# Two transformer blocks in one kernel: operands of the matrix products placed at other addresses, and sums of squares added by VectorE

## The chip, the cores and the metric

The kernel runs on one core of a Trainium2 chip. The metric is the time of one execution on the device in microseconds (us); lower is better.

## The reference

Two transformer blocks are applied to one sequence of 256 tokens with 2048 features, in fp32. Cut to what matters:

```python
# block 1
mod = silu(c) @ w_ada + b_ada                      # 6 vectors of 2048
h = rms_norm(x, mix_norm_pre) * (1 + sc1) + sh1
a_q, a_f, a_i, a_g, b_q, b_k, b_v, c_a, c_g = split(h @ w_in)
ya = hgrn2_mixer(...)                              # 8 heads, a gated recurrence
yb = dilated_attention_mixer(...)                  # 12 heads, three dilations
yc = silu(layer_norm(causal_conv31(c_a * sigmoid(c_g))))
merged = sum of sigmoid(h @ w_gate) * (y @ w_out) over the three
x = x + g1 * rms_norm(merged @ w_o, mix_norm_post)
h = rms_norm(x, mlp_norm_pre) * (1 + sc2) + sh2
x = x + g2 * rms_norm(relu(h @ w_up) ** 2 @ w_down, mlp_norm_post)
# block 2: the same frame, a context of 256 tokens beside x
# mixer: bidirectional mLSTM (8 heads) and differential attention (8 heads)
y = concat(mlstm, diff) @ w_out;  x = x + g1 * rms_norm(y, g_post_mix)
y = conv_ffn(h): three-tap convolution of h @ w_up, silu(gate) * value, @ w_down
x = x + g2 * rms_norm(y, g_post_ffn)
```

Each rms_norm needs, for every token, the sum of squares over the 2048 features; the layer norm needs the sum and the sum of squares over 768.

## The kernel before

**Layout.** Features lie on the 128 partitions, tokens along the free dimension: 2048 features are 16 tiles of 128x256. All weights come as one stream of 1 MiB blocks (16 weight tiles of 128x128, or 11 in down2) through the slots of `raw`. SyncE issues the loads in the order of `SECTIONS`, where G stands for a block of the products and A for one of the modulation (w_ada, w_mod), which VectorE multiplies and reduces itself.

**Products.** A block is split in two: ScalarE writes the high part (`split_high`, L529), VectorE the low part, weight minus high (`split_low`, L1767), both fp32r, into `parts[:, b % 2]`. The operand x also has a high and a low part. TensorE adds high x high, high x low and low x high for each tile: `product` (L1030 with the high weights, L1039 with the low ones) takes 48 matmuls of 256 columns a block. `gemm_parts` (L1066, L1069) reads both parts of x as one operand of 512 columns: 16 matmuls of 512 and 16 of 256 (11 and 11 in down2). Every matmul has its own weight load. `gemm_two`, `gate_chunk` and others are the same product in other orders; `gemm_tokens` swaps the roles, so that x is loaded and the weights stream.

**Places.** `operand` (L176) lays the fp32r operands into the arena at a given offset in fp32 elements: op_h and op_hw at 4096, merged, up1, yd and up2 at 12288, ya, yb, yc, ymh and yml between 20480 and 33024. `region` (L195) gives the arena's other pieces. `parts` and `raw` begin 128 bytes past a multiple of 512, the bytes of a weight tile in a partition, and every operand 192 past one, so 64 further.

**Sums of squares.** ScalarE squares a tile (`square_part`, L497, or `square`, L485) and TensorE multiplies by the constant matrix `ones`, which adds over the partitions and gives the sum to every partition, one fp32 matmul of 128x256 a tile, added up in PSUM. `norm` (L1134) does it at once for a finished tensor, `norm_part` (L1142) for some tiles. `root` (L492, L493) makes the reciprocal root of it. In four stages one product yields a tile (two in w_out_b), and its `norm_part` stands after the next product: w_o (into sq1), down1_3 (sqd1), w_out_b (sq2) and down2_3 (sq2). The norms of x itself (`norm_x`, with `keep_warm` around it) come in five chunks. The context's norm (`norm(sqc, KT)`) runs in down1_3. In the level stage (36 levels of the recurrence beside 43 product blocks) the convolution's mean is 6 matmuls at step 19 (L1308) and its variance `norm(squares, C_TILES)` at step 22.

**Order of the work.** Each engine's instructions are written out in its own order, with semaphores between. VectorE takes, for each block, the result of the block before from PSUM (`add_halves`, L1802 and L1803, in the down rounds; L2332 in w_out_b) and splits the block two ahead. At the end of a stage come `residual` (L1817, L1818) and `modulate_tiles`.

Of the kernel before, what the change touches and what calls it, by code (L numbers as in the profile page):

```python
# [13 lines left out]
P = 128  # L14
S = 256
# [136 lines left out]
def two_blocks_kernel(nc, stream, x_t, ctx_t, vec_d, const_d, lvl_mask_d, ident_d, rel_bias, c_rows, scratch, x_keep, out_t):  # L152
    with ExitStack() as ctx:
# [37 lines left out]
        arena = sb("arena", [P, ARENA])  # L191
# [131 lines left out]
        half_out = sem("half_out")  # L323
        dve_step, act_step = sem("dve_step"), sem("act_step")
# [144 lines left out]
        def _(act):  # L469
# [166 lines left out]
            for n in range(BESIDE_LEVELS):  # L636
# [22 lines left out]
                if s == 25:  # L659
# [132 lines left out]
            for k in range(KT):  # L792
# [6 lines left out]
                if k == 2:  # L799
                    root(rstd[:, S:512], M[2][:, 0:S], D)  # L800
                if k in (4, 6, 8, 10):
                    c = k // 2 - 2
# [205 lines left out]
        def _(pe):  # L1008
            norms, wholes, sq_parts = [0], [0], [0]
# [118 lines left out]
            def norm(src, n, sums=M[2]):  # L1128

                norms[0] += 1  # L1130
                wholes[0] += 1
                pe.wait_ge(sq_ready, wholes[0])
                for k in range(n):
                    ins = pe.matmul(sums[:, 0:S], ones[:, :], src[:, k, :], start=(k == 0), stop=(k == n - 1))  # L1134
                ins.then_inc(ms_ready, 1)

            def norm_part(src, k0, k1):
# [5 lines left out]
                if k1 == KT:  # L1143
                    norms[0] += 1
                    ins.then_inc(ms_ready, 1)

# [145 lines left out]
            for n in range(BESIDE_LEVELS):  # L1292
# [11 lines left out]
                if s == 19:  # L1304

                    pe.wait_ge(conv_tap, CONV_STEPS)
                    for t in range(C_TILES):
                        ins = pe.matmul(M[2][:, S:512], ones[:, :], cy[:, t, :], start=(t == 0), stop=(t == C_TILES - 1))  # L1308
                    ins.then_inc(mean_mm, 1)
                if s == 22:  # L1310
                    norm(squares, C_TILES)
# [108 lines left out]
            for k in range(KT):  # L1420
                gemm_T(gb("w_o", k), opG, waits={KT - 1: (merged_tile, KT)} if k == 0 else {})
                if k:
                    norm_part(sq1, k - 1, k)
            norm_part(sq1, KT - 1, KT)
# [16 lines left out]
            for k in range(KT):  # L1441
                gemm_parts(gb("down1_3", k), opU1, waits=waits if k == 0 else {})
                if k == 1:
                    norm(sqc, KT)
                if k:
                    norm_part(sqd1, k - 1, k)
            norm_part(sqd1, KT - 1, KT)
# [249 lines left out]
            for n in range(8):  # L1697
                w_out_b(n)
                if n:
                    norm_part(sq2, 2 * n - 2, 2 * n)  # L1700
            norm_part(sq2, 14, 16)
# [17 lines left out]
            for k in range(KT):  # L1719
                gemm_parts(gb("down2_3", k), opU2, kt=UP2, waits=waits if k == 0 else {})  # L1720
                if k:
                    norm_part(sq2, k - 1, k)
            norm_part(sq2, KT - 1, KT)
# [3 lines left out]
        def _(dve):  # L1727
# [103 lines left out]
            def modulate_tiles(op, u, add, n):  # L1831


                for k in range(KT + 2):
                    if k < KT:
                        scaled_tile(u, k)
                    if k >= 2:
                        low_tile(op, u, add, n, k - 2)

# [96 lines left out]
            for s in range(36):  # L1936
# [25 lines left out]
                if s == 23:  # L1962
# [4 lines left out]
                conv_taps(3)  # L1967
                dve.wait_ge(lvl_mm, s + 1)
# [99 lines left out]
            for k in range(KT - 1):  # L2068
                split_low(gb("w_o", k) + 2)
            ada_made(80)  # L2070
# [40 lines left out]
            for k in range(KT):  # L2111
# [5 lines left out]
                if k == 3:  # L2117
                    inverted()
                if k in (3, 5, 7, 9):
                    t = quarter_of(hfc, k // 2 - 1)  # L2120
                    dve.tensor_tensor(t, t, over_tiles(rstd[:, S:512], 4), ALU.mult).then_inc(cu_part, 1)
                if k in (5, 7, 9, 11):
                    c = k // 2 - 2
# [201 lines left out]
            for n in range(8):  # L2325
# [8 lines left out]
                if n < 7:  # L2334
                    split_low(b + 2)
            ada_made(176)
# [9 lines left out]
            for q in range(QUARTER):  # L2346
# [24 lines left out]
                else:  # L2371
                    if q == 3:
                        gains(mod2[:, 0, 80:96], v("g_post_ffn", 0, 16), 192)
                    add_round(f"down2_{q}", down2)
            inverted()
# [146 lines left out]
```

## Time and profile before

| what | value |
| --- | --- |
| median of 3 runs | 3223.66 us (3220.96 to 3226.57) |
| profiled execution | 3211.76 us |
| its span, first to last instruction | 3210.0 us |
| TensorE (PE) busy | 3132.3 us, 98% |
| VectorE (DVE) busy | 2345.0 us, 73% |
| ScalarE (ACT) busy | 1334.3 us, 42% |
| matmul records | 24132 |
| mean granted TensorE clock | 0.994 |
| moved by DMA | 722.63 MB |

PE is TensorE's matmuls, DVE VectorE, ACT ScalarE. A number behind L is a line of the kernel. Matmuls overlap in the pipeline, so the mean duration of one is longer than the spacing from one start to the next. An fp32 matmul of 128x256 has two records, a product's matmul (fp32r) one. The granted clock is a share of TensorE's full 2.4 GHz.

### The profile page before, as it was taken

What the parts mean: (1) busy time and instruction counts of PE and PEld (TensorE: products, weight loads), DVE (VectorE), ACT (ScalarE), POOL (GpSimd) and SP (SyncE); (2) the same over time, 40 slices, a digit from 0 to 9 for tenths busy, and PEclk for the clock granted to TensorE, in tenths of its full rate; (3) what the DMA queues carried; (4) which work ended last, traced back from release to release, by engine and by line L of the source; (5) the groups of instructions that cost most, each with busy time, mean ns of one, the idle gap of its engine ahead of it and who ended that gap; (6) DMA issues with size and microseconds to landing.
All of it is one profiled execution on the core that took longest, in us unless ns stands there. A gap on an engine that the chain in (4) does not pass through costs nothing.

```text
span 3210.0 us, 55608 instructions
## 1 busy us (share of the span) xinstructions
PE 3132.3 (98%) x24132; PEld 2962.3 (92%) x24132; DVE 2345.0 (73%) x2785; ACT 1334.3 (42%) x1459; POOL 1.8 (0%) x10
## 2 busy tenths in 40 slices
PE   7999999999999999999999999999999999999998
PEld 6899999899999999999988998989889999898997
DVE  5798866688877889899857765644757666767765
ACT  3333344444444443333463334422455444343444
POOL 0000000000000000000000000000000000000000
PEclk9999999999999999999999999999999999999999
DMA  9864444498894887777745763354343475655743
GB/s 395 328 218 158 159 148 153 170 351 340 333 349 158 305 310 272 267 265 288 287 171 192 280 257 140 139 207 158 132 145 130 169 266 193 231 207 195 248 175 118
DMA packets 106417, 722.63 MB, mean 225 GB/s; under 512 B 11677, under 2 KB 15389, under 8 KB 27197
## 3 DMA queue, kind: packets, MB, share of 16 engines
q1 hardware_dynamic: 100368, 703.64, 59.0%
q10 hardware_dynamic: 5806, 15.43, 1.6%
q8 instruction: 191, 3.13, 0.4%
q14 instruction: 52, 0.43, 0.0%
HBM read 712.41 MB, written 6.55 MB: 224 GB/s over the span
## 4 chain that ended last, share of the span: by engine, by line
PE 91%; DVE 6%; ACT 1%; DMA 1%; issue 1%; ACTq 0%; DVEq 0%
PE gemm L1030 40%; PE gemm L1039 19%; PE gemm L1066 12%; PE gemm L1069 6%; PE mix L1142 1%; DVE sb_parts L1767 1%; PE mix L1030 1%; PE mix L1269 1%; PE mix L1553 1%; DMA sb_arena<-x_t 1%; PE gemm L1185 1%; DVE sb_arena L1822 1%; PE mix L1039 1%; ACT sb_parts L529 1%; PE gemm L1619 0%
## 5 line engine op out<-in xcount | busy, mean ns | idle before, releaser
L529 ACT ACTIVATE sb_parts<-sb_raw 128x2048 fp32r<-128x2048 f32 (+2 forms) x489 | 899.6, 1842 | 1504.6 <-PE gemm L1039 964.5
L1767 DVE TENSOR_TENSOR sb_parts<-sb_raw,sb_parts 128x2048 fp32r<-128x2048 f32 (+2 forms) x489 | 1072.1, 2194 | 309.3 <-PE gemm L1039 147.2
L1030 PE MATMUL gemm<-op_h,sb_parts 128*128 128x256 f32 x7232 | 874.0, 278 | 1.1 <-ACT sb_parts L529 0.6
L1030 PEld LDWEIGHTS gemm<-op_h,sb_parts 128*128 128x128 f32 x7232 | 850.9, 188 | 2.5 <-ACT sb_parts L529 1.0
L1039 PE MATMUL gemm<-op_h,sb_parts 128*128 128x256 f32 x3616 | 453.7, 278 | 0.0
L1066 PE MATMUL gemm<-op_up,sb_parts 128*128 128x512 f32 x1728 | 424.8, 396 | 11.7 <-DVE op_up L2361 11.7
L1039 PEld LDWEIGHTS gemm<-op_h,sb_parts 128*128 128x128 f32 x3616 | 433.3, 188 | 0.2 <-DVE sb_parts L1767 0.2
L1066 PEld LDWEIGHTS gemm<-op_up,sb_parts 128*128 128x128 f32 x1728 | 318.8, 189 | 75.8 <-DVE op_up L2361 13.5
L1069 PEld LDWEIGHTS gemm<-op_up,sb_parts 128*128 128x128 f32 x1728 | 221.0, 190 | 10.6
L1748 DVE CUSTOM_DVE_ANT_0 sb_raw<-sb_raw,sb_arena,sb_vec 128x2048 f32<-128x2048 f32 x96 | 224.4, 2348 | 1.5 <-DMA sb_raw<-stream 0.2
L1069 PE MATMUL gemm<-op_up,sb_parts 128*128 128x256 f32 x1728 | 223.5, 280 | 0.0
L1030 PE MATMUL gemm<-op_hw,sb_parts 128*128 128x256 f32 (+1 forms) x992 | 174.3, 333 | 0.4 <-ACT sb_parts L529 0.4
L1030 PEld LDWEIGHTS gemm<-op_hw,sb_parts 128*128 128x128 f32 x992 | 150.3, 188 | 20.2 <-ACT sb_parts L529 0.6
L1740 DVE CUSTOM_DVE_ANT_0 sb_raw<-sb_raw,sb_arena,sb_vec 128x2048 f32<-128x2048 f32 x64 | 149.8, 2345 | 0.0
L2352 DVE SCALAR_TENSOR_TENSOR sb_arena<-gemm,sb_vec,sb_arena 128x255 f32<-128x255 f32 x88 | 42.5, 483 | 135.5 <-ACT sb_arena L981 135.5
L1030 PE MATMUL gemm<-sb_parts,op_hw 128*128 128x256 f32 x1024 | 121.6, 281 | 1.4 <-ACT sb_parts L529 1.4
L1030 PEld LDWEIGHTS gemm<-sb_parts,op_hw 128*128 128x128 f32 x1024 | 120.3, 191 | 2.6 <-ACT sb_parts L529 1.6
L1802 DVE TENSOR_TENSOR sb_arena<-gemm,sb_arena 128x256 f32<-128x256 f32 x96 | 40.6, 423 | 98.6 <-PE gemm L1069 98.5
L1039 PE MATMUL gemm<-op_hw,sb_parts 128*128 128x256 f32 (+1 forms) x496 | 89.6, 333 | 0.0
L1039 PEld LDWEIGHTS gemm<-op_hw,sb_parts 128*128 128x128 f32 x496 | 75.8, 188 | 9.9
L1142 PE MATMUL mix<-sb_arena,sb_ones 128*128 128x256 f32 x256 | 70.1, 393 | 9.5 <-ACT sb_arena L497 9.3
L1747 DVE CUSTOM_DVE_ANT_0 sb_arena<-sb_raw,sb_arena,sb_vec 128x2048 f32<-128x2048 f32 x32 | 75.0, 2345 | 0.0
(353 smaller groups left out, 3386.7 us busy)
## 6 DMA issues: line engine op xcount, KB each, us to landing
sb_raw<-stream SPq DMA_DIRECT2D x597, 1024.0 KB, 5.0
sb_raw<-stream SPq DMA_DIRECT2D x64, 704.0 KB, 4.1
sb_arena<-stream SPq DMA_DIRECT2D x14, 1024.0 KB, 8.7
sb_arena<-stream SPq DMA_DIRECT2D x10, 768.0 KB, 8.6
sb_raw<-stream SPq DMA_DIRECT2D x6, 768.0 KB, 7.6
sb_arena<-c_rows ACTq DMA_DIRECT2D x3, 1024.0 KB, 8.5
bias_rows<-sb_arena ACTq DMA_DIRECT2D x1, 2304.0 KB
sb_arena<-x_t ACTq DMA_DIRECT2D x4, 512.0 KB, 19.1
```

Of the source, the lines that this page charges most:

```text
L529: act.activation(parts[:, b % 2, 0, 0:kt, :], slot_of(slot)[:, 0:kt, :], ACT.Copy).then_inc(hi_ready, 1)
L1030: ins = pe.matmul(out, l, r, start=(opens and i == 0 and x is xh), stop=False, skip_group_check=True)
L1039: ins = pe.matmul(out, l, r, start=False, stop=(i == len(terms) - 1), skip_group_check=True)
L1066: pe.matmul(out, parts[:, b % 2, 0, k, :], op[:, :, k, :], start=(k == 0), stop=False, skip_group_check=True)
L1069: ins = pe.matmul(bank(b)[:, 0:S], parts[:, b % 2, 1, k, :], op[:, 0, k, :], start=False, stop=(k == kt - 1), skip_group_check=True)
L1142: ins = pe.matmul(M[1][:, 0:S], ones[:, :], src[:, k, :], start=(k == 0), stop=(k == KT - 1))
L1740: dve.tensor_tensor_reduce(w, w, c1_row, 1.0, v("b_ada", a), ALU.mult, ALU.add, mod1[:, a:a + 1])\
L1747: step(dve.tensor_tensor_reduce(products, w, cctx_row, 1.0, v("b_mod", a), ALU.mult, ALU.add, mod2[:, 1, a:a + 1]))
L1748: dve.tensor_tensor_reduce(w, w, c2_row, 1.0, v("b_mod", a), ALU.mult, ALU.add, mod2[:, 0, a:a + 1])\
L1767: dve.tensor_tensor(parts[:, b % 2, 1, 0:kt, :], slot_of(slot)[:, 0:kt, :], parts[:, b % 2, 0, 0:kt, :].bitcast(F32), ALU.subtract).then_i ...
L1802: step(dve.tensor_tensor(acc, bank(b)[:, 0:S], acc, ALU.add))
L2352: step(dve.scalar_tensor_tensor(y[:, 1:S], src[:, 0:S - 1], w0, y[:, 1:S], ALU.mult, ALU.add))
```

## The change

Two things are changed. `placed` moves everything in the arena: operands at 4096 and above by 16 elements (64 bytes), at 12288 and above by 48 (192 bytes), so that lower operands begin 128 and upper ones 256 bytes past a multiple of a weight tile's 512 bytes, counted from `parts`. And VectorE adds squares before TensorE sees them. In w_o, down1_3, w_out_b and down2_3 `add_square` adds each new tile's squares (two tiles in w_out_b) to the first, all but the last tile's; `norm_sum` then multiplies by `ones` twice (four times in w_out_b) after the last product. `fold` halves a tensor until one tile is left, for the context's norm and for the convolution's mean and variance, and `norm_folded` is one matmul. The steps behind these move by two positions: the root and scaling of the convolution from step 23 to 25 and its silu from 25 to 27, the context's root in down1_3 from k = 2 to 4, and the scaling and splits of the context by two blocks. The last down round is written out in a loop of its own, with `gains` ahead of it as before.

```diff
+        def placed(at):
+            return at + (48 if at >= 12288 else 16 if at >= 4096 else 0)
         def operand(name, at, *dims):
-            with nc.sbuf_tensor("pad_" + name, [P, at], F32), nc.sbuf_tensor("op_" + name, [P, *dims], F32R) as t:
+            with nc.sbuf_tensor("pad_" + name, [P, placed(at)], F32), nc.sbuf_tensor("op_" + name, [P, *dims], F32R) as t:
-        arena = sb("arena", [P, ARENA])
+        arena = sb("arena", [P, placed(ARENA)])
-            flat = arena[:, at:at + n]
+            flat = arena[:, placed(at):placed(at) + n]
...
@@ scalar
-                if s == 23:
+                if s == 25:
                     act.preload_act_table_set(LN_EXP)
                     root(rstd[:, 0:S], M[2][:, 0:S], C_TILES * P)
-                if k == 2:
+                if k == 4:
                     root(rstd[:, S:512], M[2][:, 0:S], D)
...
@@ tensor
-            def norm(src, n, sums=M[2]):
+            def norm_folded(src, n):
                 norms[0] += 1
-                for k in range(n):
-                    ins = pe.matmul(sums[:, 0:S], ones[:, :], src[:, k, :], start=(k == 0), stop=(k == n - 1))
+                pe.wait_ge(folded, n)
+                pe.matmul(M[2][:, 0:S], ones[:, :], src[:, 0, :], start=True, stop=True).then_inc(ms_ready, 1)
...
+            def norm_sum(src, width, n_parts):
+                sum_adds[0] += n_parts - 2
+                sq_parts[0] += n_parts
+                pe.wait_ge(sq_sum, sum_adds[0])
+                for k in range(width):
+                    pe.matmul(M[1][:, 0:S], ones[:, :], src[:, k, :], start=(k == 0), stop=False)
+                pe.wait_ge(sq_part, sq_parts[0])
+                for k in range(KT - width, KT):
+                    ins = pe.matmul(M[1][:, 0:S], ones[:, :], src[:, k, :], start=False, stop=(k == KT - 1))
...
                 if s == 19:
-                    pe.wait_ge(conv_tap, CONV_STEPS)
-                    for t in range(C_TILES):
-                        ins = pe.matmul(M[2][:, S:512], ones[:, :], cy[:, t, :], start=(t == 0), stop=(t == C_TILES - 1))
+                    pe.wait_ge(folded, 1)
+                    pe.matmul(M[2][:, S:512], ones[:, :], squares[:, 0, :], start=True, stop=True).then_inc(mean_mm, 1)
-                if s == 22:
-                    norm(squares, C_TILES)
+                if s == 24:
+                    norm_folded(squares, 2)
...
             for k in range(KT):
                 gemm_parts(gb("down2_3", k), opU2, kt=UP2, waits=waits if k == 0 else {})
-                if k:
-                    norm_part(sq2, k - 1, k)
-            norm_part(sq2, KT - 1, KT)
+            norm_sum(sq2, 1, KT)
...
@@ vector
+            def fold(dst, src, n):
+                while n > 2:
+                    rest = n // 2
+                    step(dve.tensor_tensor(dst[:, 0:rest, :], src[:, 0:rest, :], src[:, n - rest:n, :], ALU.add))
+                    src, n = dst, n - rest
+                dve.tensor_tensor(dst[:, 0, :], dst[:, 0, :], dst[:, 1, :], ALU.add).then_inc(folded, 1)
+            def add_square(sq, width, k, seen):
+                dve.wait_ge(sq_part, seen + k + 1)
+                if k > 1:
+                    dve.wait_ge(sq_sum, sum_adds[0])
+                sum_adds[0] += 1
+                dve.tensor_tensor(sq[:, 0:width, :], sq[:, 0:width, :], sq[:, width * k:width * (k + 1), :], ALU.add).then_inc(sq_sum, 1)
...
+                if s == 17:
+                    dve.wait_ge(conv_tap, CONV_STEPS)
+                    fold(squares, cy, C_TILES)
+                if s == 23:
+                    dve.wait_ge(sq_ready, 1)
+                    fold(squares, squares, C_TILES)
...
+                if k == 0:
+                    dve.wait_ge(sq_ready, 2)
+                    fold(sqc, sqc, KT)
+                if 1 <= k < KT - 1:
+                    add_square(sqd1, 1, k, 25)
```

TensorE in down2_3, the stage's last products (mix1 is the PSUM bank of the sums, gemm0 to gemm3 those of the products). Before:

```order
L1142 MATMUL mix1<-sb_arena,sb_ones 128x256
L1066 MATMUL gemm1<-op_up2,sb_parts 128x512 x11
L1069 MATMUL gemm1<-op_up2,sb_parts 128x256 x11
L1142 MATMUL mix1<-sb_arena,sb_ones 128x256
L1066 MATMUL gemm2<-op_up2,sb_parts 128x512 x11
L1069 MATMUL gemm2<-op_up2,sb_parts 128x256 x11
L1142 MATMUL mix1<-sb_arena,sb_ones 128x256 x2
```

And of the change, where L1073 and L1076 are the product's lines and L1159 and L1162 those of `norm_sum`:

```order
L1073 MATMUL gemm1<-op_up2,sb_parts 128x512 x11
L1076 MATMUL gemm1<-op_up2,sb_parts 128x256 x11
L1073 MATMUL gemm2<-op_up2,sb_parts 128x512 x11
L1076 MATMUL gemm2<-op_up2,sb_parts 128x256 x11
L1159 MATMUL mix1<-sb_arena,sb_ones 128x256
L1162 MATMUL mix1<-sb_arena,sb_ones 128x256
```

The matmul between two blocks is gone, and behind the last product there are two as before.

VectorE at the same place, from the 13th block on. Before:

```order
L1802 TENSOR_TENSOR sb_arena<-gemm0,sb_arena 128x256
L1803 TENSOR_TENSOR sb_arena<-gemm0,sb_arena 128x256
L1767 TENSOR_TENSOR sb_parts<-sb_raw,sb_parts 128x1408
L1802 TENSOR_TENSOR sb_arena<-gemm1,sb_arena 128x256
L1803 TENSOR_TENSOR sb_arena<-gemm1,sb_arena 128x256
L1802 TENSOR_TENSOR sb_arena<-gemm2,sb_arena 128x256
L1803 TENSOR_TENSOR sb_arena<-gemm2,sb_arena 128x256
```

Of the change, where L1811 and L1812 are the half adds, L1776 the low split and L1867 `add_square`:

```order
L1811 TENSOR_TENSOR sb_arena<-gemm0,sb_arena 128x256
L1812 TENSOR_TENSOR sb_arena<-gemm0,sb_arena 128x256
L1776 TENSOR_TENSOR sb_parts<-sb_raw,sb_parts 128x1408
L1867 TENSOR_TENSOR sb_arena<-sb_arena 128x256
L1811 TENSOR_TENSOR sb_arena<-gemm1,sb_arena 128x256
L1812 TENSOR_TENSOR sb_arena<-gemm1,sb_arena 128x256
L1867 TENSOR_TENSOR sb_arena<-sb_arena 128x256
L1811 TENSOR_TENSOR sb_arena<-gemm2,sb_arena 128x256
L1812 TENSOR_TENSOR sb_arena<-gemm2,sb_arena 128x256
```

Each tile's half adds are followed by the low split two blocks ahead and then by the add of the tile's squares; the last tile has none.

## Rows read from the trace of the kernel before

**Rows 1.** The page, part 1: busy time and share of each engine.
```profile
PE 3132.3 (98%) x24132; PEld 2962.3 (92%) x24132; DVE 2345.0 (73%) x2785; ACT 1334.3 (42%) x1459; POOL 1.8 (0%) x10
```

**Rows 2.** The page, part 4: the chain that ended last, by engine.
```profile
PE 91%; DVE 6%; ACT 1%; DMA 1%; issue 1%; ACTq 0%; DVEq 0%
```

**Rows 3.** TensorE's groups by shape: line, operands, shape, count | busy, mean ns of one.
```profile
L1066 PE MATMUL gemm<-op_up,sb_parts 128*128 128x512 f32 x1728 | 424.8, 396 | 11.7 <-DVE op_up L2361 11.7
...
L1142 PE MATMUL mix<-sb_arena,sb_ones 128*128 128x256 f32 x256 | 70.1, 393 | 9.5 <-ACT sb_arena L497 9.3
```

**Rows 4.** Timeline of TensorE, up1_0 and up1_2: start us, length us, instructions, count.
```profile
1000.90 3.93 PE L1030 MATMUL gemm<-op_h,sb_parts 128*128 128x256 f32 x32
...
1403.05 3.79 PE L1030 MATMUL gemm<-op_h,sb_parts 128*128 128x256 f32 x32
```

**Rows 5.** Timeline of TensorE, down1_0.
```profile
1090.82 3.82 PE L1066 MATMUL gemm<-op_up,sb_parts 128*128 128x512 f32 x16
1094.48 2.05 PE L1069 MATMUL gemm<-op_up,sb_parts 128*128 128x256 f32 x16
...
1100.04 1.98 PE L1069 MATMUL gemm<-op_up,sb_parts 128*128 128x256 f32 x16
```

**Rows 6.** TensorE by stretch, slow ones: from:to, length, busy (records), clock, DMA share, GB/s.
```profile
109.00:231.00 122.00, 117.77 (x1057) 1.00 0.71 244
323.00:580.00 257.00, 251.92 (x2063) 0.99 0.42 150
863.00:957.00 94.00, 94.00 (x775) 1.00 0.93 349
...
2247.00:2563.00 316.00, 308.41 (x2429) 0.99 0.40 144
2800.00:2956.00 156.00, 151.37 (x1203) 0.99 0.54 195
```

**Rows 7.** TensorE by stretch, token-major products of d_v.
```profile
2199.00:2213.00 14.00, 14.00 (x119) 1.00 0.76 291
2224.00:2238.00 14.00, 14.00 (x126) 1.00 0.81 301
```

**Rows 8.** Timeline of TensorE, down1_3: the context norm.
```profile
1605.71 7.07 PE L1134 MATMUL mix<-sb_arena,sb_ones 128*128 128x256 f32 x32
```

**Rows 9.** Timeline of TensorE: warming matmuls before the norm of x.
```profile
2420.38 4.63 PE L1151 MATMUL mix<-sb_ones 128*128 128x128 f32 x40
```

**Rows 10.** The chain in order of time, end of down2_3: start us, length us, what.
```profile
3188.96 1.29 PE gemm L1069 x11
3190.26 0.43 PE mix L1142 x2
...
3195.45 0.42 ACT sb_arena L497
...
3195.92 0.71 PE mix L1142 x2
```

**Rows 11.** VectorE's groups by shape; L1740 is a modulation column.
```profile
L1767 DVE TENSOR_TENSOR sb_parts<-sb_raw,sb_parts 128x2048 fp32r<-128x2048 f32 x419 | 958.1, 2288 | 307.4 <-PE gemm L1039 147.2 <-ACT sb_parts L529 134.9 <-DVE sb_arena L2353 17.7
...
L1740 DVE CUSTOM_DVE_ANT_0 sb_raw<-sb_raw,sb_arena,sb_vec 128x2048 f32<-128x2048 f32 x64 | 149.8, 2345 | 0.0
...
L1803 DVE TENSOR_TENSOR sb_arena<-gemm,sb_arena 128x256 f32<-128x256 f32 x96 | 40.8, 425 | 3.3
...
L1945 DVE TENSOR_TENSOR sb_arena<-sb_arena 128x512 f32<-128x512 f32 x32 | 22.2, 693 | 1.1
...
L1818 DVE TENSOR_TENSOR sb_arena<-sb_arena 128x1024 f32<-128x1024 f32 x12 | 14.7, 1225 | 0.4
```

**Rows 12.** TensorE by stretch: w_o and down1_0.
```profile
880.00:950.00 70.00, 70.00 (x579) 1.00 0.96 360
1068.00:1157.00 89.00, 89.00 (x520) 1.00 0.96 363
```

**Rows 13.** Timeline of VectorE, level stage; the idle time before it in brackets.
```profile
361.26 2.29 DVE L1767 TENSOR_TENSOR sb_parts<-sb_raw,sb_parts 128x2048 fp32r<-128x2048 f32 x1 [1.36 <-ACT sb_parts L529]
```

More of the change, by code:

```diff
@@ L323, in two_blocks_kernel @@
         half_out = sem("half_out")
+        sq_sum, folded = sem("sq_sum"), sem("folded")
         dve_step, act_step = sem("dve_step"), sem("act_step")
@@ L798, in _ @@
                 gained(down1, k)
-                if k == 2:
+                if k == 4:
                     root(rstd[:, S:512], M[2][:, 0:S], D)
-                if k in (4, 6, 8, 10):
-                    c = k // 2 - 2
+                if k in (6, 8, 10, 12):
+                    c = k // 2 - 3
                     act.wait_ge(cu_part, c + 1)
@@ L1008, in _ @@
         def _(pe):
-            norms, wholes, sq_parts = [0], [0], [0]
+            norms, sq_parts, sum_adds = [0], [0], [0]
             def product(b, pieces, it=0, dn=0, pair=False, later=False, waits={}, ready={}):
@@ L1145, in norm_part @@
                     ins.then_inc(ms_ready, 1)
+            def norm_sum(src, width, n_parts):
[7 more added lines that the diff above has]
+                    ins = pe.matmul(M[1][:, 0:S], ones[:, :], src[:, k, :], start=False, stop=(k == KT - 1))
+                norms[0] += 1
+                ins.then_inc(ms_ready, 1)
             def keep_warm(n):
@@ L1442, in _ @@
                 gemm_parts(gb("down1_3", k), opU1, waits=waits if k == 0 else {})
[L1443 to L1447, printed above, removed]
+                if k == 3:
+                    norm_folded(sqc, 3)
+            norm_sum(sqd1, 1, KT)
             def context_part(i, ks, part, xs):
@@ L2069, in _ @@
                 split_low(gb("w_o", k) + 2)
+                if k >= 1:
+                    add_square(sq1, 1, k, 4)
             ada_made(80)
@@ L2116, in _ @@
                     split_low(b + 2)
-                if k == 3:
+                if k == 0:
[3 more added lines that the diff above has]
+                    add_square(sqd1, 1, k, 25)
+                if k == 5:
                     inverted()
-                if k in (3, 5, 7, 9):
-                    t = quarter_of(hfc, k // 2 - 1)
+                if k in (5, 7, 9, 11):
+                    t = quarter_of(hfc, k // 2 - 2)
                     dve.tensor_tensor(t, t, over_tiles(rstd[:, S:512], 4), ALU.mult).then_inc(cu_part, 1)
-                if k in (5, 7, 9, 11):
-                    c = k // 2 - 2
+                if k in (7, 9, 11, 13):
+                    c = k // 2 - 3
                     dve.wait_ge(c_hi, c + 1)
@@ L2335, in _ @@
                     split_low(b + 2)
+                if 1 <= n < 7:
+                    add_square(sq2, 2, n, 46)
             ada_made(176)
@@ L2370, in _ @@
                     first_round("down2_0", down2, KT)
-                else:
-                    if q == 3:
-                        gains(mod2[:, 0, 80:96], v("g_post_ffn", 0, 16), 192)
+                elif q < 3:
                     add_round(f"down2_{q}", down2)
+            gains(mod2[:, 0, 80:96], v("g_post_ffn", 0, 16), 192)
+            for k in range(KT):
+                b = gb("down2_3", k)
+                done(dve, b)
+                add_halves(down2[:, k, :], b)
+                split_low(b + 2)
+                if 1 <= k < KT - 1:
+                    add_square(sq2, 1, k, 59)
             inverted()
```

17 lines of the change are left out of this document (5 added, 12 removed).

## Prediction

> **What bounds the kernel now.** I read the page's shares first. TensorE is busy 98% of the span [rows 1], and the chain that ended last runs through it for 91% [rows 2]. So time is taken off by giving TensorE less to do, or the same at a closer spacing; another engine matters where it makes TensorE wait. The granted clock is 0.99 to 1.00 in the stretches read [rows 6, 7, 12], the 2.4 GHz level, so it is no lever.
>
> Next comes the work itself. The products number 19,593 matmuls of 256 moving columns and 2,448 of 512 (1,728 of these in one group [rows 3]; the others are the key and context products), each with a weight load of its own. A busy time says little of pipelined matmuls, so I take the spacing of their starts: a merged timeline row, less the last one's duration, over the count less one. In up1_0, 32 products take (3.93-0.28)/31 = 0.1177 us each; the same line in up1_2 takes (3.79-0.28)/31 = 0.1132 us [rows 4]. I call them the slow and the fast pace, 117.8 and 113.3 ns. Nothing in the code tells the two stretches apart, and neither does the clock. In down1_0 the low passes take 118 and 113 ns in turn, while the 512-column products between them take (3.82-0.39)/15 = 0.229 us [rows 5]. Reading start by start, 9,461 products stand at the slow pace and 10,132 at the fast; five stretches hold most of the slow ones, 7,527 records with some others between [rows 6].
>
> For comparison, the plain fp32 matmuls of the norms: a record of the context norm starts (7.07-0.38)/31 = 215.8 ns after the last [rows 8]. It stands for half a matmul, 512 columns streamed at 4 bytes, 13 ns less than a 512-column product. So something slows the products that doesn't slow these.
>
> **Part 1, squares.** A norm matmul on the path takes 0.43 us: the chain shows it between two blocks of down2_3, 0.43 us after 1.29 us of low pass and before the next block [rows 10]; two records of 216 ns say the same. The counts that leave the stretch between the first and the last product of a stage: w_o 14 (parts 0 to 13; part 14 runs after the last product, while TensorE waits for the last square), down1_3 14, down2_3 14, w_out_b 12 (parts 0 to 5 of two tiles), the context norm 15 of 16, and the convolution's mean and variance 5 of 6 each, 10. That is 79 matmuls x 0.43 = **-34.0 us**. The end of each stage stays: halves, square of the last tile, last matmul, root. After the last product of down2_3 the chain is VectorE, then ScalarE at 3195.45, then TensorE 0.71 us from 3195.92 [rows 10]; the matmul over the summed squares runs inside that wait, as the 15th part does now.
>
> What it adds is VectorE work: 42 adds of 128x256 at 0.425 us, 6 of 128x512 at 0.693, one fold of 16 tiles (2048 columns 2.29, 1024 1.23, then 0.69 and 0.43, 4.6 us) and two of 6 tiles (768 columns about 0.96, between the neighbours, then 0.43 twice, 1.8 us each) [rows 11]: 17.9+4.2+4.6+3.6 = 30.3 us. In down2_3 VectorE has two half adds of 0.43, a low split of 2.29x11/16 = 1.6 and now another 0.43, 2.9 us beside 3.8 us of TensorE; in down1_3 3.6 beside 5.5. An add waits for the square of its own tile, which ScalarE ends before the low split is through, so what is queued behind it (the next tile's halves, and the low split two blocks ahead) isn't late. The add of tile 14 has no split to cover it in down2_3, but the last product does. In w_o VectorE also has about one modulation column of 2.35 us a block [rows 11]: 2.29+2.35+0.43 = 5.1 beside 5.7. The level stage is tighter: VectorE is idle 1.36 us a level there [rows 13], and the second fold takes 1.8, so some tenths may show once. I cost all this at 0; its cover is TensorE's block time, and without cover it would be at most +30.3 us, which is a rival below.
>
> **Part 2, placement.** Only addresses change. Weight tiles (512 bytes a partition, beginning at 128 modulo 512) keep their place; each operand and the arena's parts move from 64 bytes past that to 128 (op_h, op_hw) or 256 (merged, up, yd, ya, yb, yc). No instruction is added. TensorE reads a weight tile and a moving operand at the same time, so their relative place could set how often they meet, but no row shows another placement for these products: everything in the trace stands 64 past. One thing the rows exclude: that the moving operand's own start decides. In the token-major products the weights' side moves, from parts, and the operand is loaded; the same two paces appear there (119 records in 14 us, then 126 in 14 us [rows 7]).
>
> So I bound it from both sides. Best end: every product streams like the fp32 records, 108 ns for 256 columns and 215.8 for 512: 10,132x5.3 + 9,461x9.8 + 2,448x13 = 54+93+32 = -179 us. Worst end that a row gives: all 256-column products at the slow pace, 10,132x4.5 = +46 us. The value I take is the nearest row, the fast pace that the same instruction already shows in half its cases: 9,461x4.5 = -42.6 us, 512 columns unchanged. Of that some can't be cashed. In w_o and down1_0 each product comes with a modulation block, two 1 MiB transfers; the DMA engines are 96% busy at 360 and 363 GB/s [rows 12], so a pair can't come faster than 2.1 MB/(363/0.96) = 5.55 us. w_o's block falls from 6.09 to 5.66 by part 1, and the fast pace would make it 5.44: 0.11x16 = 1.8 us are lost, about 1 more in down1_0. Part 2: **-40 us**.
>
> TensorE: Matmul & The Clock Gate, in the Trainium skill, says in its part on what happens when a matmul is issued that TensorE has two independent SBUF read ports, and that loading the next weights takes no read bandwidth from the running matmul. By that rule placement does nothing, and the sum would be the squares alone. The trace doesn't settle it: the products' extra 13 ns speak against it, the unexplained switching between paces fits either.
>
> **Sum.** -34-40 = -74 us. The profiled execution took 3211.76 us (span 3210.0), so it would take 3138. The median of the runs, 3223.66, is 11.9 above the profiled one; I take the difference over to it: 3150.
>
> **Rivals.**
> Only the squares. Placement doesn't reach TensorE's pace, or it reshuffles slow and fast stretches. For it: the pace changes now at unchanged addresses [rows 4, 5]. Against: the 13 ns. Time: 3223.7-34 = 3190.
>
> Both reads run free. Placement ends the cause behind both paces and behind 229 ns: 512 columns at 215.8 (-32), 256 columns at 111.6, which is what the warming matmuls show, (4.63-0.28)/39, where every 256 streamed columns bring one weight load [rows 9]: 10,132x1.7+9,461x6.2 = -76. With the squares -142: 3082. For it: those two rows reach these spacings with the same array and clock. Against: they are fp32 and may read differently.
>
> Slower. The new relative place is the worse one and holds every 256-column product at the slow pace: +46-34 = +12, 3235. It turns at a mean spacing of 115.5+34/19,593 = 117.2 ns over all these products; over 117.6 it counts as slower. For it: up2_0, up2_2 and w_o already stay slow throughout. Against: half of the stretches aren't.
>
> VectorE shows through. The added 30.3 us aren't hidden, at the level stage, w_o and the context fold first, while placement gains as forecast: 3150+30 = 3180. Against: VectorE is busy 73% [rows 1] and TensorE was its releaser before most of its idle time.
>
> **How the numbers follow.** Forecast 0.36, only squares 0.22, both free 0.22, slower 0.10, VectorE 0.10. A measurement here tells about 0.2%, 6.4 us, from no change. Forecast, squares, free and VectorE all lie over 6.4 us below, 0.90; of the slower case a third lies within 6.4 us, 0.03, and the rest is slower, 0.07. The range goes from 3078, which takes in the free case's own centre, to 3205, which takes in the squares with part of VectorE's work showing; outside are the slower case and the lower half of the free one. The likeliest case's own range is 3125 to 3175.
>
> **What would show it.** Right: 0.43 us gone between blocks of w_o, down1_3 and down2_3, with the same chain behind each stage's last product; 128x256 adds on VectorE behind each low split, and no new idle time of TensorE by them; 32 products in 3.79 us in up1_0 and up2_0; 512 columns still at 229. Only squares: rows of 3.93 us remain in about half the stretches. Free: 16 products of 512 columns in about 3.6 us. Slower: rows of 3.93 or more in merge and up1_1. The prediction is wrong in its kind if TensorE waits for the new sums inside a stage, or if the products' spacing takes a value that no row shows.

## The result, and the profile after

The change makes the kernel slower: 3245.57 us (median of 4 runs, 3243.78 to 3248.16) against 3225.11 for the kernel before, a ratio of 1.0064, 95% interval 1.0047 to 1.0082, so by little, but clear of 1. Forecast were 3150 us. The profiled execution has a span of 3241.9 us, 31.9 more than the one before.

The page, part 1, after the change:

```profile
PE 3164.0 (98%) x23974; PEld 2996.2 (92%) x23974; DVE 2371.8 (73%) x2843; ACT 1334.2 (41%) x1459; POOL 1.8 (0%) x10
```

Against [rows 1] there are 158 matmul records fewer, the two halves of 79 norm matmuls, and yet PE is busy 31.7 us longer, which is all of the difference in the span. PE's idle time is unchanged: 3210.0 - 3132.3 = 77.7 us before, 3241.9 - 3164.0 = 77.9 now. So the added time is not waiting; TensorE does less and is slower at it. TensorE's waits confirm it (engine, line, what it waited for: us in total, times, longest):

```profile
PE gemm L1073 <- DVE op_up L2405: 11.8, 4, 4.6
PE mix L1147 <- ACT sb_arena L504: 6.5, 9, 2.3
...
PE mix L1159 <- DVE sb_arena L1867: 0.8, 1, 0.8
```

In the kernel before the first two were 11.7 and 9.3 us [rows 3]. Part of the 9.3 now stands under `norm_sum`, as 2.6 us of waits for ScalarE's last squares (L1162). The third is new: at the end of w_o TensorE waits once, 0.8 us, for the summed squares.

**The squares** went as the diff says. The chain in order of time, at the end of down2_3:

```profile
3220.09 1.31 PE gemm L1076 x11
3221.41 2.52 PE gemm L1073 x11
...
3226.66 0.71 PE mix L1162 x2
```

The 0.43 us between two blocks [rows 10] are gone, and the tail is as it was: the last tile's square (0.42 us of ScalarE, up to 3226.62), then 0.71 us of matmuls, then the root. But the eleven low matmuls take 1.31 us, where 1.29 stood before.

**The spacing** is where the time is. TensorE's timeline in w_o, up1_0, up1_2 and down1_0 (start us, length us, instructions, count):

```profile
896.15 4.00 PE L1037 MATMUL gemm<-op_merged,sb_parts 128*128 128x256 f32 x32
...
1003.65 3.96 PE L1037 MATMUL gemm<-op_h,sb_parts 128*128 128x256 f32 x32
...
1092.49 2.08 PE L1076 MATMUL gemm<-op_up,sb_parts 128*128 128x256 f32 x16
...
1403.91 3.96 PE L1037 MATMUL gemm<-op_h,sb_parts 128*128 128x256 f32 x32
```

Taken as in [rows 4], 32 products of op_h, now 128 bytes past a weight tile, come at (3.96-0.28)/31 = 118.7 ns in both stretches, where 117.7 and 113.2 stood. Those of merged, 256 past, come at (4.00-0.28)/31 = 120.0, and the low passes of down1_0 at (2.08-0.28)/15 = 120.0 in every block, where 118 and 113 took turns [rows 5]. The alternation is gone, to the slow side of both. The 512-column products of up keep 229 ns, 16 of them in 3.82 us. Read start by start over the whole trace, 256-column products stand 118.9 ns apart on average, 115.5 before. 19,593 x 3.4 = +67 us, and 512 columns, 1.1 ns further apart by those of op_hw, +3; with the squares' -34 that is +36, beside 31.9 in the spans. The means over whole traces are worked out from the starts of the single matmuls; the pages don't show them.

### The profile page after: what moved, and what is told of

It reads as the page before. It is cut to its first block, busy times and chain, and to the rows that moved or that the text cites. A ratio compares the mean times of both kernels' runs of the same rounds, so it can differ in the third digit from the quotient of the medians.

```text
span 3241.9 us, 55394 instructions
## 1 busy us (share of the span) xinstructions
PE 3164.0 (98%) x23974; PEld 2996.2 (92%) x23974; DVE 2371.8 (73%) x2843; ACT 1334.2 (41%) x1459; POOL 1.8 (0%) x10
## 4 chain that ended last, share of the span: by engine, by line
PE 90%; DVE 6%; DMA 2%; ACT 1%; issue 1%; ACTq 0%; DVEq 0%
PE gemm L1037 39%; PE gemm L1046 19%; PE gemm L1073 12%; PE gemm L1076 6%; DVE sb_parts L1776 1%; PE mix L1037 1%; DMA sb_raw<-stream 1%; PE mix L1288 1%; PE mix L1566 1%; ACT sb_parts L536 1%; DMA sb_arena<-x_t 1%; DVE sb_arena L1831 1%; PE mix L1046 1%; PE gemm L1204 1%; DVE sb_arena L1887 1%
## 5 line engine op out<-in xcount | busy, mean ns | idle before, releaser
L1776 DVE TENSOR_TENSOR sb_parts<-sb_raw,sb_parts 128x2048 fp32r<-128x2048 f32 (+2 forms) x489 | 1072.2, 2194 | 313.2 <-PE gemm L1046 151.4
L1037 PE MATMUL gemm<-op_h,sb_parts 128*128 128x256 f32 x7232 | 898.4, 282 | 1.0 <-ACT sb_parts L536 0.6
L1037 PEld LDWEIGHTS gemm<-op_h,sb_parts 128*128 128x128 f32 x7232 | 874.4, 188 | 2.4 <-ACT sb_parts L536 1.0
L1046 PE MATMUL gemm<-op_h,sb_parts 128*128 128x256 f32 x3616 | 466.3, 282 | 0.0
L1046 PEld LDWEIGHTS gemm<-op_h,sb_parts 128*128 128x128 f32 x3616 | 445.1, 188 | 0.1
L1073 PE MATMUL gemm<-op_up,sb_parts 128*128 128x512 f32 x1728 | 420.2, 393 | 11.8 <-DVE op_up L2405 11.8
L1073 PEld LDWEIGHTS gemm<-op_up,sb_parts 128*128 128x128 f32 x1728 | 318.7, 190 | 74.3 <-DVE op_up L2405 13.5
L1076 PEld LDWEIGHTS gemm<-op_up,sb_parts 128*128 128x128 f32 x1728 | 226.6, 193 | 9.9
L1076 PE MATMUL gemm<-op_up,sb_parts 128*128 128x256 f32 x1728 | 229.7, 285 | 0.0
L1811 DVE TENSOR_TENSOR sb_arena<-gemm,sb_arena 128x256 f32<-128x256 f32 x96 | 40.6, 423 | 68.3 <-PE gemm L1076 68.3
L2135 DVE TENSOR_TENSOR sb_arena<-sb_arena 128x256 f32<-128x256 f32 x64 | 27.1, 424 | 69.1 <-ACT sb_arena L787 69.1
```

The source lines that it names most:

```text
L1037: ins = pe.matmul(out, l, r, start=(opens and i == 0 and x is xh), stop=False, skip_group_check=True)
L1046: ins = pe.matmul(out, l, r, start=False, stop=(i == len(terms) - 1), skip_group_check=True)
L1073: pe.matmul(out, parts[:, b % 2, 0, k, :], op[:, :, k, :], start=(k == 0), stop=False, skip_group_check=True)
L1076: ins = pe.matmul(bank(b)[:, 0:S], parts[:, b % 2, 1, k, :], op[:, 0, k, :], start=False, stop=(k == kt - 1), skip_group_check=True)
L1776: dve.tensor_tensor(parts[:, b % 2, 1, 0:kt, :], slot_of(slot)[:, 0:kt, :], parts[:, b % 2, 0, 0:kt, :].bitcast(F32), ALU.subtract).then_i ...
L1811: step(dve.tensor_tensor(acc, bank(b)[:, 0:S], acc, ALU.add))
```

## The experiments

The expectations use letters for the theories. A: the place of the moving operand against the weight tile sets the spacing. B: the norm matmuls between blocks had kept the products at the fast spacing, and without them it is lost. C: VectorE's adds make TensorE wait. A1: within A, only the distance to the nearest multiple of 128 bytes counts. A2: within A, the rounder the place the slower, so that multiples of 32 alone are best. A3: the operand's own address counts. A4: the distance to a whole weight tile counts. A5: the place decides which spacings there are, and chance which of them a stretch gets. The place is always counted from a multiple of the weight tile's 512 bytes, as `parts` has them, so the kernel before is at 64 throughout.

### Which part costs the time

**sq_only**: the squares, with every address as before.

```diff
-            return at + (48 if at >= 12288 else 16 if at >= 4096 else 0)
+            return at
```

> The change with placed returning its argument, so operands stay 64 bytes past a multiple of a weight tile. Theory A (the place relative to the weight tile sets the spacing of the products): the two paces of 113.3 and 117.8 ns come back, the 79 norm matmuls are gone, so about 34 us under the kernel before, ratio 0.989 to 0.991. Theory B (the norm matmuls between blocks kept TensorE in the fast pace, and taking them out locks it in the slow one, wherever the operands lie): nearly all products at 118 to 120 ns as in the change, ratio 1.00 to 1.007. Theory C (the added VectorE work holds TensorE up): paces as before but new idle time of TensorE, ratio 0.995 to 1.00.

**place_only**: the kernel before, with `placed` alone.

```diff
+        def placed(at):
+            return at + (48 if at >= 12288 else 16 if at >= 4096 else 0)
```

> The kernel before with the change's placement alone. Theory A: 256-column products at 118.7 to 120 ns throughout, 19,593 times 3.3 to 3.5 ns more than the mean of before, so +55 us plus or minus 8 us, ratio 1.014 to 1.020. Theory B: the norm matmuls are back, so the fast pace comes back in half the stretches, ratio 0.998 to 1.003. Theory C: as B.

Measured side by side with the kernel before (3226.21): sq_only 3192.31, ratio 0.9884 (0.9861 to 0.9906), which is -33.9 us; place_only 3279.93, ratio 1.0158 (1.0132 to 1.0184), which is +53.7. The product of the two ratios is 1.0040, the change's own 1.0064; the uncertainties of the three cover the difference. So the parts add up, and neither needs the other: B falls, since the placement costs as much with all norm matmuls in place, and C falls but for the 0.8 us above, since the squares alone gain what their matmuls are worth (33.9 us, by the interval of the ratio 30 to 45). From place_only to the change the squares bring 3279.93 - 3245.57 = 34.4 us. In sq_only the page's first part reads

```profile
PE 3111.7 (98%) x23974; PEld 2945.2 (92%) x23974; DVE 2370.9 (74%) x2843; ACT 1335.1 (42%) x1459; POOL 1.8 (0%) x10
```

which is the same count of matmuls as in the change in 52.3 us less, and an idle time of 3191.2 - 3111.7 = 79.5 us. place_only shows the change's row in up1_2, and its low passes of down1_0 take 2.08 us as well:

```profile
1403.63 3.96 PE L1033 MATMUL gemm<-op_h,sb_parts 128*128 128x256 f32 x32
```

### Which places are slow

Eight more placements, each with the squares of the change and every operand and region from 0 on at one place:

```diff
-            return at + (48 if at >= 12288 else 16 if at >= 4096 else 0)
+            return at + c
```

with c = 112 (place 0), 120 (32), 8 (96), 16 (128), 32 (192), 64 (320), 80 (384) and 96 (448).

> The change, but everything in the arena moved by 448 bytes, so that every operand begins exactly on a multiple of a weight tile. Theory A says that the spacing depends on this place and gives no value for it: anything from 109 to 125 ns, but one that differs from 113.3 and 117.8 mixed. Theory B: the same spacing as the change, within 0.3 ns, and 3240 to 3250 us.

> The change, but everything moved by 64 bytes, so that all operands begin 128 bytes past a multiple of a weight tile, the upper ones too. Theory A: 118.7 ns as the lower operands show now, also for op_up, op_merged and op_yd, which show 119.7 at 256; 512-column products of op_up go from 228.5 towards the 231 to 234 that op_hw shows at 128; 3235 to 3250 us. Theory B: no difference between this and the change in any group.

> The change with all operands 32 bytes past a multiple of a weight tile. Measured so far for 256-column products, mean spacing: 120.0 ns at 0 and at 256, 118.7 at 128, 115.4 to 116.2 at 64. Theory A1 (what counts is the distance to a multiple of 128): between the values at 0 and 64, 116 to 119 ns, 3210 to 3240 us. Theory A2 (what counts is how evenly the start divides: the rounder the number, the slower): under 115 ns, 3150 to 3185 us.

> All operands 96 bytes past a multiple of a weight tile. Theory A1: 116 to 119 ns, as at 32. Theory A2: under 115 ns, as at 32. If the streams merely have to be some distance apart inside 128 bytes, 32 and 96 differ from each other.

> All operands 192 bytes past a multiple of a weight tile. Theories A1 and A2 both say that it is like 64: the two paces of 113.3 and 117.8 ns, mean 115 to 118, 3180 to 3210 us. A theory in which the distance from the tile's start itself counts (0 bad, 64 good, farther bad) says 119 to 120 ns and 3240 to 3255 us.

> All operands 448 bytes past a multiple of a weight tile, which is 64 before the next. Theories A1 and A2: the two paces of 113.3 and 117.8 ns, 3180 to 3210 us. If it matters which of the two streams is ahead, another spacing.

> The squares as in the change, every operand and region 320 bytes past a multiple of a weight tile. Theory A1 (what counts is the distance to the nearest multiple of 128 bytes, 64 at best, and 320 is like 64, 192 and 448): 256 columns at 114.9 to 116.3 ns, 3178 to 3195. Rival A4 (the distance to a whole tile counts, and 320 lies in the middle of it like 256): 118 ns and more, 3235 to 3260.

> The squares as in the change, every operand and region 384 bytes past a multiple of a weight tile. So far 0 and 256 look alike, 64 and 320, 192 and 448. If the pattern repeats every 256 bytes, 384 is like 128: 256 columns at 118.8 ns in a spread of 115 to 122, 512 columns at 233 ns, 3245 to 3258. Rival (it does not, only the distance to a multiple of 128 counts, in which 0 and 128 differ already by chance): 512 columns at 228 as at 0, or 256 columns at 120 ns flat.

Measured, with the mean spacing of starts over each kernel's products, in ns; times are of one execution, except where a number of runs stands. They come from several chips, on which the kernel before took 3225 to 3231 us; executions of the kernels at 64 and 192 scatter by up to 25 us (below):

| place | 256 columns | 512 columns | time, us |
| --- | --- | --- | --- |
| 0 | 119.9 | 228.3 | 3256.9 |
| 32 | 117.2 | 233.3 | 3217.7 |
| 64 (sq_only) | 116.2 | 229.1 | 3192.3 (4 runs) |
| 96 | 119.8 | 233.4 | 3267.2 |
| 128 | 118.8 | 232.9 | 3251.6 |
| 192 | 114.9 | 233.0 | 3180.0 |
| 320 | 116.1 | 229.1 | 3199.3 |
| 384 | 118.8 | 232.8 | 3252.9 |
| 448 | 115.5 | 233.1 | 3193.3 |
| 128 and 256 (the change) | 118.9 | 230.1 | 3245.6 (4 runs) |

The timelines behind it, in up1 and down1_0: at 0,

```profile
1401.66 4.00 PE L1037 MATMUL gemm<-op_h,sb_parts 128*128 128x256 f32 x32
...
1101.99 3.82 PE L1073 MATMUL gemm<-op_up,sb_parts 128*128 128x512 f32 x16
```

at 96,

```profile
1087.75 2.08 PE L1076 MATMUL gemm<-op_up,sb_parts 128*128 128x256 f32 x16
```

at 192,

```profile
1398.95 3.79 PE L1037 MATMUL gemm<-op_h,sb_parts 128*128 128x256 f32 x32
...
1102.52 3.89 PE L1073 MATMUL gemm<-op_up,sb_parts 128*128 128x512 f32 x16
```

and at 384:

```profile
1104.47 3.88 PE L1073 MATMUL gemm<-op_up,sb_parts 128*128 128x512 f32 x16
```

Theory A holds: nothing but addresses differs, and the times follow the spacings from 3180 to 3267 us; of 0 and 96, nearly equal in 256 columns, the one with 512 columns at 233 ns is the slower. At 0 and at 256 (merged and up in the change) the 256-column products stand at 120 ns flat and those of 512 columns in 3.82 us; at 128 and 384 256 columns spread over 115 to 122 ns and 512 columns take 3.88. A4 falls at 320, which is like 64, not like 256. A1 holds for the 256-column products of the multiples of 64 (the odd ones stand at 114.9 to 116.2, the even ones at 118.8 to 119.9), but not for 512 columns, where 64 and 320 have 229 and 192 and 448 have 233, nor for 32 and 96, which are equally far from a multiple of 128 and stand at 117.2 and 119.8. A2 falls: 32 and 96 should have been the best places. What is left is plainer than any of them: every pair 256 bytes apart that was measured (64 and 320, 192 and 448, 128 and 384, 0 and the change's upper operands) has the same two numbers within 0.6 ns, so the pattern repeats every 256 bytes. Not all single forecasts were met: 128 came out 1.6 us above its range, 320 4.3 us above A1's, and 96, which A1 had at 116 to 119 ns, at 119.8.

### Relative place, or the operand's own

**sq_pad**: the squares with the old offsets, and 64 bytes ahead of all tensors.

```diff
+        sb("front", [P, 16])
         raw = sb("raw", [P, SLOTS, KT, P])
...
-            return at + (48 if at >= 12288 else 16 if at >= 4096 else 0)
+            return at
```

> The squares alone with the old offsets, but 64 bytes are put in front of everything: the weight tiles, the other small tensors and the arena all move by 64 bytes, so every operand keeps 64 bytes past a weight tile, while its own start goes from 192 to 256 modulo 512, where the placement at 128 has it. Theory A (the distance between operand and weight tile counts): 3192, 256 columns at 116.2 ns, 512 columns at 229. Rival A3 (the operand's own address counts, whatever the weight tile's): as with every operand 128 past, 3252, 256 columns at 118.8 ns, 512 columns at 233.

Measured: 3200.11 us beside 3231.18 for the kernel before, ratio 0.9908 (0.9879 to 0.9937); 256 columns at 116.0 ns, 512 at 229.0. Its timeline in up1_2 and down1_0:

```profile
1404.52 3.79 PE L1038 MATMUL gemm<-op_h,sb_parts 128*128 128x256 f32 x32
...
1090.47 1.98 PE L1077 MATMUL gemm<-op_up,sb_parts 128*128 128x256 f32 x16
1092.29 3.82 PE L1074 MATMUL gemm<-op_up,sb_parts 128*128 128x512 f32 x16
1095.95 2.05 PE L1077 MATMUL gemm<-op_up,sb_parts 128*128 128x256 f32 x16
```

The two spacings and their turns are back, with operands that begin where those of the kernel at 128 do (3251.6 us). The 3200 us are 8 us more than sq_only took, on another chip and with overlapping intervals, while the rival asked for 3252. A3 falls: what counts is the distance between the two. `raw` keeps its distance to `parts` in every run, so the runs don't tell a distance to the weight tile from one to `raw`; TensorE reads only the first of them in these products.

### Chance, and the best version

**sq_192_timed** and **sq_192_again** are the kernel at 192 once more, **sq_64_again** is sq_only once more. **sq_mixed** and **sq_mixed_again** put the operands of 512-column products at 64 and all others from 4096 on at 192:

```diff
-            return at + (48 if at >= 12288 else 16 if at >= 4096 else 0)
+            return at + (160 if at >= 12288 else 32 if at >= 4096 else 0)
...
+            put = at + 128 if name in ("hw", "up1", "up2") else placed(at)
-            with nc.sbuf_tensor("pad_" + name, [P, placed(at)], F32), nc.sbuf_tensor("op_" + name, [P, *dims], F32R) as t:
+            with nc.sbuf_tensor("pad_" + name, [P, put], F32), nc.sbuf_tensor("op_" + name, [P, *dims], F32R) as t:
```

> The squares as in the change, every operand and region 192 bytes past a multiple of a weight tile (counted from parts), timed against the kernel before. One look gave 3180.0 us. Theory A (the place of an operand against the weight tile sets the spacing of the products): 256 columns at 114.9 ns again, 512 columns at 233, 3175 to 3185, ratio 0.985 to 0.988, so below the squares alone at the old place (3192). Rival (the spacing of one execution is chance, and 3180 was a lucky one): the executions spread over 3180 to 3200, with a median near 3192.

> The squares as in the change; op_hw, op_up1 and op_up2, the operands whose products have 512 columns, lie 64 bytes past a multiple of a weight tile, everything else from 4096 on 192 past. Theory A, worked out from the spacings measured at 64 and at 192: from 3180.0 at 192 throughout, 512 columns 1592 x -3.8 and 689 x -4.4 ns, the token-major products of op_hw 1499 x -2.7 ns, the 256-column products of up and op_hw 1580 x +1.2 and 945 x +1.0 ns, together -10.4 us: 3170, ratio 0.983. Rival (spacings depend on the whole program, not on the operand at hand): no sum of this kind holds, 3180 to 3192.

> The squares alone at the old place (64 past), once more, beside the same squares at 192 on one chip. Theory A5 (the place decides which two spacings there are, 113.3 and 117.8 ns at every odd multiple of 64, and an execution falls into one or the other by chance at TensorE's pauses, staying for up to 2,400 products): the mean is 115.0 to 117.0 ns again, but the stretches that are slow are not those of the first time; median 3188 to 3198, single executions up to 12 us apart. Rival (64 is a worse place than 192 by 6 us): the median is 5 us or more above that at 192.

> The squares at 192 past, once more. Theory A5: the two spacings and the mix by chance as at 64, 512 columns at 233 instead of 229 ns (+10 us), so no better than at 64 by more than its share of fast stretches brings: 3182 to 3196. Rival (192 keeps the products at the fast spacing more often): 3175 to 3188, and at least 5 us under the run at 64 beside it.

> The mixed placement (operands of 512-column products 64 past, the rest 192), once more. Theory A5: as at 192 less 10 us for the 512 columns at 229 ns, less or more what chance gives: 3178 to 3192, ratio 0.984 to 0.989. If the rival of the run at 192 holds, it is the fastest of the three; otherwise it lies within 5 us of the run at 64.

| kernel | median (runs), us | ratio, 95% interval | 256 / 512 columns, ns |
| --- | --- | --- | --- |
| sq_192_timed | 3188.87 (6) | 0.9870 (0.9844 to 0.9896) | 115.5 / 233.1 |
| sq_mixed | 3186.08 (4) | 0.9862 (0.9837 to 0.9888) | 115.9 / 229.1 |
| sq_64_again | 3194.91 (6) | 0.9885 (0.9858 to 0.9912) | 116.3 / 229.0 |
| sq_192_again | 3188.39 (6) | 0.9871 (0.9843 to 0.9899) | 115.8 / 233.1 |
| sq_mixed_again | 3181.26 (6) | 0.9852 (0.9822 to 0.9882) | 115.6 / 229.1 |

Two executions of one kernel differ by up to 25 us here (at 192: 3176.29 to 3201.02), so the 3180.0 of the single execution at 192 was a lucky one: the two medians are 3188.9 and 3188.4, above theory A's 3175 to 3185. The profile says where executions differ. Window 620 to 850 us, the merge products, of sq_only and of sq_64_again, which are the same kernel (from:to, length, busy (records), clock, DMA share, GB/s):

```profile
620.00:850.00 230.00, 230.00 (x2032) 1.00 0.89 342
```

```profile
620.00:850.00 230.00, 230.00 (x1955) 1.00 0.85 329
```

230 us over 2,032 records are 113.2 ns each, over 1,955 they are 117.6. The same stretch of the same program stands at the fast spacing throughout in one execution and at the slow one in the other. So A5 holds in that chance decides about whole stretches. What picks one of them for a stretch was not found.

A5's ranges for the medians of the three kernels on one chip were met. But chance is not all. The rival expected the kernel at 64 to be 5 us or more above the one at 192 beside it: it is 6.5 us above (3194.91 and 3188.39, the latter at the edge of the rival's own 3175 to 3188). A mixed placement ahead of both was to be the sign of the same rival, and it is ahead, 13.7 us under the kernel at 64: five of its six runs took 3175.4 to 3183.7 us, five of six at 64 took 3193.1 to 3197.3. On the other chip it is 14.0 us under sq_pad, the kernel there whose operands stand at 64, and none of its four runs (3182.1 to 3192.0) reaches the fastest of sq_pad's four (3195.6). All of these have 512 columns at 229 ns, one row of down1_0 of sq_mixed_again:

```profile
1100.59 3.84 PE L1074 MATMUL gemm<-op_up,sb_parts 128*128 128x512 f32 x16
```

So what separates them is the 256-column products: their mean is 115.9 and 115.6 ns in the mixed kernel's two profiled executions and 116.0 to 116.3 in the squares at 64 and 320. That odd multiples of 64 differ in their share of fast stretches is therefore likely, but not shown from the traces: the kernel before stands at 64 too, and its one profiled execution, a fast one, has 115.5. Over the kernel at 192 the mixed one gains 2.8 and 7.1 us, of some 10 that 512 columns at 229 instead of 233 ns are worth, with runs that overlap. Its sum of spacings, 3170, was missed, since a fast stretch of one execution is not owned by a place: op_hw, expected at 115.8, had 117.8 in sq_mixed, and merged 113.6. That this kernel beats both the kernel before and the changed one is certain.

At the fast spacing another limit shows. In w_o of sq_mixed a block takes 5.44 us, from 910.67 to the next one's start at 916.11, until the weights are late:

```profile
910.67 3.79 PE L1038 MATMUL gemm<-op_merged,sb_parts 128*128 128x256 f32 x32
...
922.68 3.90 PE L1038 MATMUL gemm<-op_merged,sb_parts 128*128 128x256 f32 x32 [0.96 <-ACT sb_parts L537]
```

ScalarE had waited 3.64 us for the stream before it wrote that block's high part, and the DMA engines were 99% busy at 378 GB/s from 894 to 950 us. From 894.07 to 944.95 nine blocks take 5.65 us each, no less than 48 products at the slow spacing (5.65), so in this stage the fast one gains nothing.

## Why the prediction was wrong

**What bounds the kernel.** Right: TensorE's time is the kernel's time, at a granted clock of 0.99 to 1.00 before and after, and what the change did to the spacing arrived in the span.

**The squares, -34.0.** Right, in size and in kind: -33.9 from the kernel before to sq_only, -34.4 from place_only to the change. VectorE's 30.3 us, costed at 0, cost next to nothing: it is busy 26.8 us more [rows 1], and the adds are there (groups by shape, of after):

```profile
L1867 DVE TENSOR_TENSOR sb_arena<-sb_arena 128x256 f32<-128x256 f32 x42 | 17.6, 419 | 0.5 <-ACT sb_arena L504 0.5
```

The 42 adds of one tile waited 0.5 us in all for a square. In the level stage, the tight place, VectorE is still idle 1.39 us a level, and the first fold, 1.41 us and then one add of 0.42, follows a low split before which VectorE had been idle 2.31 us.

What the step missed is small: the last add of w_o stands behind a low split, and that one behind a block of the stream that came late, so TensorE waited for it 0.8 us in the change, 1.05 in sq_only and 1.4 in the kernel at 192 that ran once.

**The placement, -40.** This step failed, in sign. Measured alone it is +53.7. Three things were wrong in it. The value taken, "the nearest row, the fast pace", was a row of the same instruction at the same place; it says what the old place can do, and nothing of a new one. The worst end, +46 with every product at 117.8, was taken as a bound because no row was slower; but the premise of the step was that the place sets the spacing, and under it rows of one place bound nothing. The changed kernel shows 118.7 and 120.0, and place 96, by its time, costs still more: "a value that no row shows", which the text had named as what would make it wrong in its kind. And 512 columns, left at 229, moved too: op_hw at 128 stands at 233 ns.

The exclusion in that step, that the operand's own start doesn't decide, is confirmed by sq_pad. The reading of 216 ns for fp32 matmuls as the speed without interference has something for it: they don't care for the place. Sixteen records of the norm of x take 3.72 us in the kernels before, of the change and at place 96; the row at 96:

```profile
2468.06 3.72 PE L1147 MATMUL mix<-sb_arena,sb_ones 128*128 128x256 f32 x16 [0.40 <-ACT sb_arena L504]
```

But no placement brought the fp32r products there, and the rival with both reads free falls with that.

By the rule of two independent read ports (the Trainium skill, TensorE: Matmul & The Clock Gate, on what happens when a matmul is issued) placement would do nothing. This case's runs disagree: 32 bytes more or less of distance between the two operands move the kernel by up to 75 us (64 to 96), at the same instructions and at a clock of 0.993 and 0.994. No run tells how many ports there are; the speed of these products is not independent of where their two operands lie to each other.

**The rivals.** The slower one had the mechanism and the right turning point: the mean, 118.9 ns, is beyond 117.6. Its price was too small by 1.1 ns a product, some 20 us, of which the median's own mix of spacings (below) gives about half back, and so its 3235 lies 10 us under the result. It had a chance of 0.10. The argument against it, that half the stretches weren't slow before, was again a fact about the old place. "Only the squares" is what sq_only measures, 3192 for a forecast of 3190. The one in which VectorE shows through falls by PE's idle time. The limit by the DMA engines in w_o and down1_0, 5.55 us a block, didn't come up in the change, whose blocks of w_o take 5.76 us; it is real, as w_o of sq_mixed shows (above).

**Over to the median.** The profiled execution before lay 11.9 us under the median, and this was carried over as it stood. It is, most likely, the mix of the two spacings, though no execution at the median was profiled: 115.5 ns in that execution, 116.0 to 116.3 in the squares at the same place, and 19,593 x 0.6 = 12 us. The difference of two profiled spans has that much chance in it: sq_only's span is 18.8 under that of before, its median 33.9; place_only's span is 67.9 above it, its median 53.7.

## What to carry to other kernels

If a change moves operands to an address at which nothing in the trace stands, its effect has no row and its range must be open on both sides; a fast stretch that the same address shows is no evidence for the new one. In a kernel of back-to-back fp32r products with a weight load each, the moving operand did best at an odd multiple of 64 bytes from the weight tiles; start there and measure two or three places, for from the median at 192 to the worst place it was 78 us of 3200. A single execution can be 10 us beside its median. Sums of squares added by an engine with idle time, so that TensorE adds over the partitions only once, gained what their matmuls had cost, within the scatter.

## What the runs showed of the hardware

The spacing of fp32r matmuls with a weight load each depends on the distance between the moving operand and the weight tile in a partition, modulo 256 bytes as far as four pairs of places show. At 0 it is 120 ns for 256 columns, at 128 it spreads over 115 to 122, at 96 it has a mean of 119.8. At 64 and 192 there are two, 113.3 and 117.8, and a stretch of products holds one of them, differently in two executions of the same kernel. For 512 columns its mean is 228 to 229 ns at 0 and 64, and 233 at 32, 96, 128 and 192. Plain fp32 matmuls, at 216 ns a record, show none of this at 64, at 96 and in the change. Why it is so, no run tells.
